# Routing the first layer in two parts: the sequence's top-k between the context tiles' steps, the context's beside expert 0

## The reference, cut to what matters

```python
def expert_choice_ffn(h, router, w_gate, w_up, w_down):
    bsz, t, d = h.shape
    cap = CAPACITY_FACTOR * t // N_EXPERTS          # 64 for the sequence, 32 for the context
    aff = jax.nn.softmax((h @ router).astype(jnp.float32), axis=-1)
    gates, idx = lax.top_k(jnp.swapaxes(aff, 1, 2), cap)
    xs = jax.vmap(lambda hb, ib: hb[ib])(h, idx)
    a = jnp.einsum('becd,edf->becf', xs, w_gate)
    u = jnp.einsum('becd,edf->becf', xs, w_up)
    y = jnp.einsum('becf,efd->becd', jax.nn.silu(a) * u, w_down)
    ...
# in layer(): x and xc are routed and added apart
    x_new = x_new + g2 * expert_choice_ffn(h2, router, w_gate, w_up, w_down)
    if need_ctx:                                    # layer 0 only
        xc = xc + cg2 * expert_choice_ffn(hc2, router, w_gate, w_up, w_down)
```

## Time and profile before

| | |
|---|---|
| median of the runs (three) | 3226.77 us (3226.46 to 3227.11) |
| profiled execution, its own time | 3225.97 us |
| its span, first to last instruction | 3224.2 us |
| TensorE busy | 2992.5 us (93%) |
| VectorE / ScalarE / GpSimd busy | 1085.3 / 724.6 / 382.0 us |
| DMA | 626.97 MB, mean 194 GB/s |
| granted clock of TensorE, mean | 0.962 of full speed |

### The profile page before, as it was taken

How to read it: one execution, slowest core, us unless ns; L and a number is a source line. 1 busy time by engine, 2 the same in 40 slices (tenths; PEclk the granted TensorE clock), 3 DMA queues, 4 the chain that set the end, 5 groups by cost and what they waited for, 6 DMA issues and landing times.

```text
span 3224.2 us, 50144 instructions
## 1 busy us (share of the span) xinstructions
PE 2992.5 (93%) x21722; PEld 1863.4 (58%) x21722; DVE 1085.3 (34%) x1912; ACT 724.6 (22%) x1375; POOL 382.0 (12%) x494
## 2 busy tenths in 40 slices
PE   6999989699999998986988988999999999999999
PEld 3645545445454474544433333888875568678887
DVE  4124733211111254633222224322424473232242
ACT  3113641000000132530000002222323262222232
POOL 2022520112122121411100000000000000000000
PEclk9998989799999999987999999999999999999999
DMA  8930032899999810036999997122212012231230
GB/s 348 393 121 1 1 144 99 332 401 406 411 406 412 335 55 0 1 131 257 415 423 423 423 423 287 59 105 79 98 58 79 35 52 79 78 111 62 69 139 32
DMA packets 138400, 626.97 MB, mean 194 GB/s; under 512 B 12592, under 2 KB 19776, under 8 KB 82896
## 3 DMA queue, kind: packets, MB, share of 16 engines
q1 hardware_dynamic: 122064, 577.67, 44.7%
q0 software_dynamic: 16128, 46.18, 4.3%
HBM read 607.36 MB, written 16.45 MB: 193 GB/s over the span
## 4 chain that ended last, share of the span: by engine, by line
PE 49%; DMA 10%; DVE 3%; ACT 1%; issue 1%; SPq 0%; POOL 0%; DVEq 0%; ACTq 0%; POOLq 0%
PE bank L932 21%; PE bank L1484 7%; DMA slots<-in_w_up_dram 7%; PE bank L1672 4%; DMA slots<-in_w_gate_dram 3%; PE bank L1361 3%; PE bank L1588 3%; PE bank L1070 2%; PE bank L1250 2%; PE bank L1182 1%; PE bank L1605 1%; PE bank L1203 1%; PE bank L1382 1%; PE bank L1616 0%; PE bank L1411 0%
## 5 line engine op out<-in xcount | busy, mean ns | idle before, releaser
L1361 PE MATMUL bank<-slots,HT 128*32 128x256 f32 x8192 | 484.1, 388 | 50.9 <-DMA slots<-in_w_gate_dram 26.8
L1361 PEld LDWEIGHTS bank<-slots,HT 128*32 128x32 f32 x8192 | 269.0, 112 | 270.3 <-issue 73.7
L932 PE MATMUL bank<-hT_high,chunk_high 128*128 128x512 f32 (+2 forms) x736 | 285.4, 388 | 6.2 <-DVE hT_low L2442 6.2
L932 PE MATMUL bank<-hT_high,low_slots 128*128 128x512 f32 (+2 forms) x736 | 287.3, 390 | 0.0
L932 PE MATMUL bank<-hT_low,chunk_high 128*128 128x512 f32 (+2 forms) x736 | 285.8, 388 | 0.0
L2033 ACT ACTIVATE arena<-bank 128x512 f32<-128x512 f32 x32 | 19.2, 599 | 759.4 <-PE bank L1361 436.4
L932 PE MATMUL bank<-slots,HT 128*128 128x512 f32 (+4 forms) x544 | 178.8, 488 | 7.2 <-issue 5.8
L2769 DVE TENSOR_TENSOR arena<-bank,arena 128x512 f32<-128x512 f32 x32 | 22.1, 692 | 441.4 <-ACT arena L2033 441.4
L932 PEld LDWEIGHTS bank<-hT_high,chunk_high 128*128 128x128 f32 x736 | 139.2, 189 | 36.8 <-DVE hT_low L2442 6.4
L932 PEld LDWEIGHTS bank<-hT_low,chunk_high 128*128 128x128 f32 x736 | 139.0, 189 | 32.2 <-issue 0.2
L932 PEld LDWEIGHTS bank<-hT_high,low_slots 128*128 128x128 f32 x736 | 138.9, 189 | 29.5
(11 more groups left out here) (437 smaller groups left out, 4762.7 us busy)
## 6 DMA issues: line engine op xcount, KB each, us to landing
slots<-in_w_gate_dram SPq DMA_DIRECT2D x128, 1024.0 KB, 20.5
slots<-in_w_up_dram SPq DMA_DIRECT2D x128, 1024.0 KB, 22.5
arena<-in_w_down_dram SPq DMA_DIRECT2D x80, 1024.0 KB, 25.7
arena<-in_ada_w_dram SPq DMA_DIRECT2D x48, 1024.0 KB, 9.5
X<-in_w_down_dram SPq DMA_DIRECT2D x32, 1024.0 KB, 17.9
slots<-in_w_in_dram SPq DMA_DIRECT2D x15, 2048.0 KB, 10.2
slots<-in_ffn_w_gate_dram SPq DMA_DIRECT2D x10, 2048.0 KB, 7.9
slots<-in_ffn_w_up_dram SPq DMA_DIRECT2D x10, 2048.0 KB, 8.9
```

The costliest lines, as they stand in the source:

```text
L932: mm = pe.matmul(out_, lhsT, rhs, start=(n == 0), stop=(n == len(pairs) - 1))
L1361: mm = pe.matmul(bank[32 * j:32 * j + 32, 2 + n, 256 * g:256 * g + 256], xT[:, 64 * k + 32 * g:64 * k + 32 * g + 32], columns(w[:, c, :], ...
```

## The change

The diff gives the sequence a routing of its own inside `w_out` of layer 0, and leaves the context's in `route` and at the start of `experts`.

- TensorE in `w_out`: the router product of tile 3 goes between the two halves of tile 5's projection; the transposes of the sequence's affinities (bank 7) stand behind the turning of tile 4, and those of its lists (bank 3) behind the last router product. The context's affinities are turned in `route`, its lists between quarters 1 and 2 of expert 0.
- VectorE in `w_out`: a generator `rank_sequence` does softmax, transposed copy and rounds; three rounds are drawn before tile 5's product is awaited, one in the middle of tile 5, two before its turned rows are copied, the rest behind. In `route_both` it makes the sequence's indices, the context's softmax, two rounds, the copy of expert 0's rows, the last two rounds and the context's indices.
- ScalarE: the exponential of the sequence in `w_out`, with a load of the exponential's table before it and of the root's after.
- Expert 0 on TensorE: all four quarters of the sequence, then turning the context's rows, then the four context quarters, each of which signals `gu_read`. TensorE doesn't wait for the others' end of `route`.
- GpSimd: the sequence's four gathers first, gate rows and token ids, then the context's two gathers.
- SP: the first down pieces wait for the last row of `w_out`, not for VectorE's end of it. This holds in both layers. Otherwise layer 1's routing is the same work through the new helpers.

```diff
-                sp.wait_ge(sem["vector_finished"], stage.facts["arena_free"])
+                sp.wait_ge(sem["rows_ready"], projected.at("rows_ready", projected.signals["rows_ready"]))
                 load_down(1, 1)
-                sp.wait_ge(sem["logits"], projected.at("logits", 1))
+                sp.wait_ge(sem["logits"], projected.at("logits", projected.signals["logits"]))
...
+            def turn_affinities(st, ctx):
+
+                b = (7, 1)[ctx]
+                lanes = slice(C_LANE, C_LANE + EXPERTS) if ctx else slice(0, HALF_LANE + EXPERTS)
+                pe.wait_ge(sem["affinity"], st.at("affinity", ctx + 1))
+                pe_may_fill(pe, st, b, 0)
+                for u in range(2):
+                    mm = pe.transpose(bank[0:lanes.stop - lanes.start, b, tile_cols(u)], aff_lanes[:, u, lanes], ident[:, :])
...
+                if tiles > ST:
+                    for i in range(ST):
+                        project_tile(i + 1)
+                        turn_rows(i)
+                        if i:
+                            logits(i - 1)
+                    project_tile(ST + 1, between=lambda: logits(ST - 1))
+                    turn_rows(ST)
+                    turn_affinities(stage_behind(st), 0)
+                    logits(ST)
+                    turn_rows(ST + 1)
+                    logits(ST + 1)
+                    turn_pairs(stage_behind(st), 0)
+                    return
                 for i in range(tiles):
...
+                    routed = stages[st.number - 1]
+                    pe.wait_ge(sem["gathered0"], gathered(0))
+                    turn_sequence(0)
+                    pe.wait_ge(sem["x_done"], st.at("x_done", 1))
+                    pe.wait_ge(sem["free3"], routed.at("bank3", 1))
+                    for q in range(4):
+                        gate_up_sequence(0, q)
+                        if q == 1:
+                            turn_pairs(routed, 1)
+                    pe.wait_ge(sem["context_gathered"], 16)
+                    turn_context_rows(0)
                     pe.wait_ge(sem["c_done"], st.at("c_done", 1))
-                for q in range(4):
-                    gate_up(0, q)
...
+                    if i == ST and tiles > ST:
+                        step(act.activation(junk[:, 0:1], eps[:, :], ACT.Exp))
+                        exponentials(stage_behind(st), 0)
+                        step(act.activation(junk[:, 0:1], eps[:, :], ACT.Sqrt))
...
+                    if i == ST + 1:
+                        some_ranking(3)
...
+                    if i == ST + 1:
+                        some_ranking(1)
...
+                some_ranking(2)
                 take_turned(tiles - 1)
+                some_ranking(None)
...
+            def rank_sequence(st):
+
+                lanes = slice(0, HALF_LANE + EXPERTS)
+                step(dve.memset(aff_lanes[:, :, :], 0.0))
+                affinities(st, 0)
+                dve.wait_ge(sem["full7"], at_bank(st, 7, 0))
+                dve.tensor_copy(affT[lanes, :], bank[lanes, 7, 0:HALF]).then_inc(sem["free7"], 1)
+                dve.wait_ge(sem["free7"], at_bank(st, 7, 0))
+                yield from ranked_rounds(affT[lanes, :], top[lanes, :], places[lanes, :], CAP_X // 8)
+                merge_sequence()
...
+            def route_both(st):
+
+                index_sequence(st)
+                affinities(st, 1)
+                first = slice(0, EXPERTS)
+                dve.wait_ge(sem["full1"], at_bank(st, 1, 0))
+                dve.tensor_copy(affT_c[first, :], bank[first, 1, 0:HALF]).then_inc(sem["free1"], 1)
+                dve.wait_ge(sem["free1"], at_bank(st, 1, 0))
+                rounds = ranked_rounds(affT_c[first, :], top_c[first, :], places_c[first, :], CAP_C // 8)
+                next(rounds)
+                next(rounds)
+                take_rows(stage_behind(st), 0)
+                for _ in rounds:
+                    pass
+                dve.tensor_copy(pair_at[first, 3, :].rearrange("p (a n) -> p a n", a=4), again(places_c[first, :], 4))
+                dve.tensor_copy(pair_gate[first, 1, :].rearrange("p (a n) -> p a n", a=4), again(top_c[first, :], 4))\
+                   .then_inc(sem["ranked"], 1)
+                dve.wait_ge(sem["full7"], at_bank(st, 7, 1))
+                turned = bank[:, 7, 0:6 * EXPERTS].rearrange("p (a n) -> p a n", n=EXPERTS)
+                rows_of(turned, 2, 1, 3, 4, 1).then_inc(sem["indexed"], 1)
+                rows_of(turned, 4, 1, 3, 2, 3)
+                dve.tensor_copy(last_c, turned[:, 3, EXPERTS - 1:EXPERTS])
...
-                    gather([index[:, n, half:half + 1] for n in range(kinds)], half)
+                    gather([index[:, n, half:half + 1] for n in range(2)], half)
...
+                    pool.wait_ge(sem["indexed"], stages[st.number - 1].at("indexed", 2))
+                    for half, name in enumerate(("context_gathered", "gathered1")):
+                        pool.indirect_dma_start(xs_c[:, half, 0:256], None, rows, bass.IndirectOffsetOnAxis(ap=index[:, 2, half:half + 1], axis=0))\
+                            .then_inc(sem[name], 16)
```

More of the change, by code:

```diff
@@ L318, in block_one_stages @@
         for half in range(2):
-            own[f"gathered{half}"] = (3 if both else 2) * 8 * EXPERTS
+            own[f"gathered{half}"] = (3 if both else 2) * 8 * EXPERTS - (16 if both and half == 0 else 0)
+        if both:
+            own["context_gathered"] = 16
         if both:
@@ L1278, in project_tile @@
                     for j in range(2):
+                        if j and between is not None:
+                            between()
                         if i >= 2:
@@ L1320, in route @@
                 pe_may_fill(pe, st, 3, 0)
-                turned = [(n, pair_at[0:EXPERTS, n, :]) for n in ((0, 1, 2, 3) if both else (0, 1, 2))]
-                turned += [(4 + n, pair_gate[0:EXPERTS, n, :]) for n in range(2 if both else 1)]
+                turned = [(n, pair_at[0:EXPERTS, n, :]) for n in range(3)] + [(4, pair_gate[0:EXPERTS, 0, :])]
                 for n, rows in turned:
@@ L1353, in gate_up, with gate_up_sequence @@
                 def gate_up(e, q):
+                    mm = gate_up_sequence(e, q)
+                    if both:
+                        mm = gate_up_context(q)
+                    mm.then_inc(sem["gu_read"], 1)
+                def gate_up_sequence(e, q):
                     for n in range(2):
@@ L1702, in _ @@
             for st in stages:
-                if st.name in programs and st.name not in ("ada", "join", "join_two", "conv_in", "ffn_down", "latent_qk", "route"):
+                held_open = st.name == "experts" and st.layer == 0
+                if st.name in programs and not held_open \
+                        and st.name not in ("ada", "join", "join_two", "conv_in", "ffn_down", "latent_qk", "route"):
                     enter(pe, st)
@@ L2711, in route @@
-                first, second, context = slice(0, EXPERTS), slice(HALF_LANE, HALF_LANE + EXPERTS), slice(C_LANE, C_LANE + EXPERTS)
-                def again(v, count):
-                    return v.unsqueeze(1).broadcast_to([EXPERTS, count, v.shape[-1]])
-                at_x = slot_at[first, :]
-                step.later(dve.tensor_copy(second_top[first, :], top[second, ::-1]))
-                step.later(dve.tensor_scalar(at_x, places[second, ::-1], float(HALF), None, ALU.add))
-                step.later(dve.tensor_copy(first_at[first, :], places[first, :]))
@@ L2726, in route @@
[L2726 to L2731 removed]
+                for _ in ranked_rounds(affT[0:lanes, :], top[0:lanes, :], places[0:lanes, :], CAP_X // 8):
+                    pass
@@ L2820, in turn @@
                     outcome(e, half)
-                take(0)
+                if not both:
+                    take(0)
                 product_of(0, 0)
@@ L3285, in gather @@
                 def gather(at, half):
-                    for n in range(kinds):
+                    for n in range(len(at)):
                         dst = xs[:, half, 256 * n:256 * n + 256] if n < 2 else xs_c[:, half, 0:256]
```

203 lines of the change are left out of this document (130 added, 73 removed).

## The result

The changed kernel takes 3234.01 us (median of 20 runs, 3227.47 to 3244.58) against 3227.61 for the kernel before beside it: a ratio of 1.002, 95% interval 1.0011 to 1.0028. Two further series gave 1.0015 (0.9998 to 1.0032) and 1.0017 (1.0002 to 1.0031). So it is slower by about 0.2%, where 0.1% faster was forecast, and outside the range. One of the 20 runs of the kernel before took 6569.28 us and has no part in the ratio. The other runs of one kernel differ by up to 22 us and go with their mean granted clock (0.955 to 0.967, the lower the longer), so a few us are read from places inside the traces.

The account below looks back on a forecast made before the run. TensorE and the weight stream run side by side, the later ending the stage. Each allowed 3.9 us earlier, of which 3.4 was kept: 3226.77 to 3223.4 us, range 3219.5 to 3229.

Parts of the forecast that it names:

- Router product, softmax, transposes, tile 5's delay, indices: First layer's output projection: sequence logits at 551.1, softmax hidden, transposes at 559.1, tile 5's row 9.0 us late, indices at 581.3.
- The first gather: GpSimd before expert 0: waits for indices and tile 5's stores, between 582.1 and 584.2 us, taken as 583.
- I am wrong if: Failure signs: first gather waiting past 586 on stores, TensorE pausing between expert 0's parts, or dry stretch after 592 over 20 us.
- The gather's landing: Sequence rows before expert 0: 5.5 us after the second gather's issue, at 589.9 (bounds 586.3 to 592.1).
- Expert 0's sequence quarters: TensorE, gate and up: four of 3.45 us plus 1.7 for low clock and 0.3, from 592.0 to 607.8.
- Turn, copy and context quarters: Expert 0 after the sequence: 1.1 us for turn and copy, then context quarters from 608.9 to 615.8.
- The context's cover: Context's gather lands at 604.9 beside expert 0's sequence quarters, 2.9 us early, so it costs nothing.
- rival 2: Context's gather arrives late before expert 0's context quarters, costing 2 to 8 us, 3229 to 3235; chance 0.08.
- The weight stream: First layer's expert loads: margin 2.0 us at expert 14, stream 1.9 us earlier, so stage ends at most 3.9 earlier.
- second dry stretch: DMA engines nearly idle from 627.5 to 632 us, 4.5 us; it vanishes because expert 1 starts early enough.
- Layer 1: Its routing only written anew; TensorE waits for weights throughout and passes the first layer's shift on unchanged.
- Rival 1: Weight loads take the gain: first layer's experts end 1 us earlier to 2 later, 3225.5 to 3229; chance 0.22.

Follow-up runs that it names:

- Experiments 2 and 3: Changed kernel with sequence gathers not awaiting tile 5's stores (0.9973 of before); or layer 0's first down pieces issued behind those stores (0.9956; on another chip 1.0).
- e11: Changed kernel with tile 5's product ahead of the top-k rounds and layer 0's first down pieces behind tile 5's stores: 3227.46 us, 0.9995 of before.

## Why the prediction failed, point by point

- **Router product, softmax, transposes, tile 5's delay, indices: right.** The last router product of the sequence starts at 550.09 and ends near 552 (forecast 551.1), tile 5's residual starts at 564.96 (564.7), its row is stored from 572.48 (572.4), the indices are made at 580.40 (581.3). This trace runs 0.8 us late against that of before.
- **The first gather: the step that failed first.** The first gather is at 586.49; less the 0.8 us by which this execution ran late, that is 2.7 us later than the 583 of the forecast. 0.7 of it is a slip: "I take the full value, 583.7" for the landing, and 583 for the gather that has to wait for it. 0.9 is the store: it was issued 0.8 earlier than reckoned but took 12.4 us, and 10.7, the largest in the earlier trace rows, was no bound (the unchanged kernel's other two profiles have 11.2 and 12.3). 1.1 us lie between the landing and the gather, GpSimd's own steps, which had no term. Experiments 2 and 3 show that the store is what holds the gather, and that the down pieces, which the change lets go at that very moment, are what delays the store: 3.7 us without them. I had seen that they start together and took one reading as the worst case. The mark set under "I am wrong if", a first gather past 586, was passed (by 0.5 us in this trace; 585.7 with the 0.8 taken off).
- **The gather's landing: mis-sized.** 8.6 us from the first gather to the turning of the rows where 6.9 was taken, 1.7 more. The full stage's value was the right neighbour, not one in between.
- **Expert 0's sequence quarters: mis-sized.** 613.78 - 597.02 = 16.8 us against 15.8; the clock is 0.85 in these 16.8 us, where the first 16.8 us of expert 0 before had 0.90. Turn, copy and context quarters were right (8.1 against 8.0).
- These make 2.7 + 1.7 + 1.0 = 5.4 us, less 0.1. The end of expert 0 was to be 3.9 us earlier and is 1.4 later.
- **The context's cover: right.** Its rows needed no wait at 613.78; rival 2 did not occur.
- **The weight stream: right in kind.** The second dry stretch is gone, TensorE waits 1.3 us at expert 14. Its first load came 5.2 us later than forecast, with expert 0. Its start of 612.8 lies 2.0 us behind the issue at 610.8, for which no row is given. Expert 3's last up piece landed at 695.7 (forecast 688.7, before 690.6), expert 14's at 1063.3, when TensorE reads it: the margin of 2.0 us is gone. Instead of 3.4 us earlier, down 15 is 3.2 us later on the mean of three profiles: 1.6 by TensorE's start at expert 1, 1.4 by the waits on weights, 0.2 left over. The join, 2.5 later, hides a part of that.
- **Layer 1: wrong.** "it passes the shift on unchanged" does not hold for the clock ahead of its attention: 2.0 us, which the forecast did not have. Why the clock falls there and not in the kernel before is open. Whether the experts of layer 1 pass a shift on was not looked at by itself.
- **Rival 1's sum: wrong in one step.** It calls the bound 592.1 "1 later than I took"; that is 2.2 later than 589.9 (1.2 of it the gather at 584.2, 1.0 the landing).
- **The sum.** 2.5 + 2.0 = 4.5 us (4.4 by the marks at the attention) of a measured 5 to 6.5 (0.15 to 0.2%). The rest, 1 to 2 us, is less than the runs can tell and stays unexplained.
- The chance of slower, 0.05, was too small. The range of the store's landing (576.7 to 583.7) had its own forecast at the upper end, and nothing beyond it; rival 1, with "the store at its worst 2 more", was nearest to what happened.

## What to carry to other kernels

An operation moved ahead on a serial engine delays the one queued behind it: take the delay on to everything that the delayed instruction releases, and there to what is issued in the same microsecond by another queue. A small transfer that someone waits for goes ahead of the bulk transfers, not with them; here 4.6 us by which one queue's loads went out later were worth 6.7 us at the end of the stage. Where a bound rests on the largest landing seen, take a second profile, and ask whether more is queued in the changed kernel than was then. And where a lag of a few us is read at one mark, look at the granted clock between the marks first.

## What the runs showed of the hardware

- The landing of a store of 512 KB hangs on the loads that another queue has issued ahead of it. It took 12.4 us with 4 MB issued 0.8 us ahead; 7.5 us with 4 MB issued 7 to 9 us ahead and nothing beside it (both edits, e11); 3.7 us with the loads behind it. From 572.2 to 585.4 us of the changed kernel the DMA engines moved 352 GB/s, by my estimate 4.6 of the 5.2 MB that the four pieces and the two stores make: the store landed near the end of all that had been issued with it. Gathers of 128 KB landed 6.9 to 7.5 us after their issue with the next four down pieces under way, issued 1.0 us ahead of the first, and 2.7 to 3.9 in the earlier trace rows. The Trainium skill (DMA: Bandwidth & Descriptors, SWDGE vs HWDGE vs iDMA) has the queues taken in turn; these rows show no protection of the small transfer by that.
- On two of the four chips of the experiments TensorE needs 0.6 to 1.0 us more for each expert of layer 0 (9 to 15.5 us over the stage), in all seven profiles taken there, whatever the kernel. Its weight loads in the last context quarter come in groups of five or six with gaps that no semaphore explains, here in the run with the gathers early (in the first profile of the changed kernel the same quarter is one group of 32):

```profile
872.42 0.17 PEld L1427 LDWEIGHTS bank<-slots,HT 128*32 128x32 f32 x6 [0.37 <-issue]
873.15 0.17 PEld L1427 LDWEIGHTS bank<-slots,HT 128*32 128x32 f32 x5 [0.56 <-issue]
873.87 0.19 PEld L1427 LDWEIGHTS bank<-slots,HT 128*32 128x32 f32 x6 [0.55 <-issue]
```

- The same pause of TensorE is followed by low clock in one profile and not in another: after 2.78 us at the last expert's down in 7 of 17 profiles, after 2.2 us ahead of layer 1's first large product in 13 of 17.
- The granted clock can fall in the middle of work that is the same in each execution. The changed kernel in two profiles, 2594 to 2630 us:

```profile
2594.00:2630.00 36.00, 34.53 (x154) 21.86 (x153) 20.10 (x67) 19.68 (x54) 0.00 (x0) 0.81 0.01 1
```

```profile
2594.00:2630.00 36.00, 34.53 (x196) 23.09 (x195) 24.65 (x80) 22.46 (x63) 0.00 (x0) 1.00 0.01 1
```

The group of products that starts at 2598.57 us in the first and at 2600.20 in the second takes 26.5 and 20.2 us: the first loses 6.3 us here, the second nothing. Single profiles of two kernels can differ by that much with no cause in either.
